# Scan block of a hybrid decoder step: cached keys turned in another batch order, and their scores issued for four batches at once

## The reference, cut to what matters

```
k_ctx = jnp.concatenate([k_buf.astype(ak.dtype), ak], axis=1)    # k_buf: 8 batches x 256 past tokens x 6 heads x 64
s = jnp.einsum('bqhd,bpqjhd->bpqhj', qblk, kg).astype(f32) * scale
...
p = jnp.exp(s - lse[..., None])
o = jnp.einsum('bpqhj,bpqjhd->bpqhd', p.astype(vg.dtype), vg).astype(f32)
```

## Time and profile before

| | |
|---|---|
| median of three runs | 2490.94 us (2488.32 to 2491.29) |
| profiled execution, first to last instruction (its span; the page gives no other time of its own) | 2483.1 us |
| what lies around the span, against that median | 7.8 us |
| PE busy | 2420.2 us, 97% |
| PEld busy | 2263.6 us, 91% |
| DVE busy | 1634.5 us, 66% |
| ACT busy | 1048.3 us, 42% |
| POOL busy | 11.4 us |
| mean rate of the DMAs | 115 GB/s |
| granted TensorE clock, mean of the span | 0.991 |

### The profile page before, as it was taken

One profiled execution on the slowest core, in us unless ns is written; L12 is line 12 of the kernel. 1 busy time (PEld: TensorE's weight loads), 2 busy tenths in 40 slices (PEclk: granted clock), 3 DMA queues, 4 the chain that ended last, 5 costly groups with the idle time before them and its releaser, 6 DMA issues. The chain is left out here.

```text
span 2483.1 us, 49073 instructions
## 1 busy us (share of the span) xinstructions
PE 2420.2 (97%) x19147; PEld 2263.6 (91%) x19147; DVE 1634.5 (66%) x2830; ACT 1048.3 (42%) x1709; POOL 11.4 (0%) x43
## 2 busy tenths in 40 slices
PE   7999999999999999999999999998999999999998
PEld 5998999899877999899999989988989689999997
DVE  8872684565857786278478538726668678846854
ACT  5541353343554554145255315424247445533532
POOL 0000000000000000000000000000000000000000
PEclk8999999999999999999999999999999999999999
DMA  8246335522233224633233553364121331322331
GB/s 307 74 137 215 109 99 184 185 78 73 69 128 96 69 77 134 213 94 96 82 86 85 161 187 97 105 214 156 44 90 52 121 120 52 99 85 81 101 87 62
DMA packets 398243, 285.67 MB, mean 115 GB/s; under 512 B 18274, under 2 KB 396440, under 8 KB 397703
## 3 DMA queue, kind: packets, MB, share of 16 engines
q1 hardware_dynamic: 397676, 283.36, 37.6%
q10 hardware_dynamic: 410, 0.18, 0.0%
HBM read 271.71 MB, written 11.79 MB: 114 GB/s over the span
## 5 line engine op out<-in xcount | busy, mean ns | idle before, releaser
L347 PE MATMUL PS<-f_xH,f_wqH 128*128 128x288 f32 x2140 | 634.9, 297 | 3.1 <-issue 3.0
L347 PE MATMUL PS<-f_xL,f_wqH 128*128 128x288 f32 x2140 | 631.8, 295 | 0.0
L347 PE MATMUL PS<-f_xH,f_wqL 128*128 128x288 f32 x2140 | 629.8, 294 | 0.0
L347 PEld LDWEIGHTS PS<-f_xH,f_wqH 128*128 128x128 f32 x2140 | 401.2, 187 | 6.0 <-issue 5.4
L347 PEld LDWEIGHTS PS<-f_xH,f_wqL 128*128 128x128 f32 x2140 | 403.3, 188 | 0.0
L347 PEld LDWEIGHTS PS<-f_xL,f_wqH 128*128 128x128 f32 x2140 | 401.9, 188 | 0.0
L347 PE MATMUL PS<-f_actH,f_wqH 128*128 128x288 f32 x1408 | 323.9, 301 | 1.3 <-DVE f_wqL L1013 1.3
L347 PE MATMUL PS<-f_actH,f_wqL 128*128 128x288 f32 x1408 | 315.4, 295 | 0.0
L347 PE MATMUL PS<-f_actL,f_wqH 128*128 128x288 f32 x1408 | 315.3, 295 | 0.0
L746 DVE SCALAR_TENSOR_TENSOR xT<-PS,modT,xT 128x288 f32<-128x288 f32 (+1 forms) x80 | 41.4, 517 | 369.2 <-PE PS L347 368.9
L347 PEld LDWEIGHTS PS<-f_actH,f_wqH 128*128 128x128 f32 x1408 | 230.2, 189 | 27.0 <-issue 25.0
(11 more groups left out here) (536 smaller groups left out, 4323.6 us busy)
## 6 DMA issues: line engine op xcount, KB each, us to landing
wslot<-in_ffn_w_in SPq DMA_DIRECT2D x176, 512.0 KB, 5.1
masks<-in_w_mod SPq DMA_DIRECT2D x42, 1536.0 KB, 6.7
wslot<-in_ffn_w_out SPq DMA_DIRECT2D x64, 384.0 KB, 4.1
wslot<-in_w_in SPq DMA_DIRECT2D x48, 512.0 KB, 4.7
wslot<-in_ffn_w_out SPq DMA_DIRECT2D x64, 320.0 KB, 3.4
setup<-in_w_mod SPq DMA_DIRECT2D x6, 1536.0 KB, 12.7
wslot<-in_w_out SPq DMA_DIRECT2D x16, 512.0 KB, 4.7
dec<-in_cache_attn_k SPq DMA_DIRECT2D x16, 384.0 KB, 3.9
```

Source lines behind the costliest of these rows:

```text
L347: ins = e.matmul(outs[j], w, x_hl[j][part], start=(start and w is wh and part == 0), stop=(stop and w is wl), skip_group_check=True)
```

## The change

There are now four buffers of turned keys instead of two: the two of `KT`, and two that lie in `h0T` and `Btm`, which the scan needs only later in the block. The cached keys are loaded in the batch order 0, 2, 4, 6, 1, 3, 5, 7, so that any four in a row belong to four different quarters of the partitions. `scores` is called twice instead of eight times; each call has twelve matmuls, of four batches in turn for each j. Their number, shapes and operands are the same in total (24 per layer). The first call stands behind `turn_keys(4)`, the second where `scores(7)` stood. `keep_keys` of the fifth to eighth turned batch wait for the first call. Two steps are also moved on TensorE: `turn_x(p+1)` now comes ahead of the second `turn_keys` of an even k.

```
+            K_ORDER = [0, 2, 4, 6, 1, 3, 5, 7]
+            KEYS = [KT[:, 0], KT[:, 1], h0T.rearrange("p a n -> p (a n)").rearrange("p (j s) -> p j s", j=NJ),
+                    Btm.rearrange("p a n -> p (a n)")[:, 0:NJ * PAST].rearrange("p (j s) -> p j s", j=NJ)]
...
-                    for b in range(4, NB):
-                        e.wait_ge(sem("ky_turned"), b - 3)
-                        e.dma_start(ring[:, b % 4], cache("cache_attn_k", b)).then_inc(ring_loaded[b % 4], 16)
+                    for i in range(4, NB):
+                        e.wait_ge(sem("ky_turned"), i - 3)
+                        e.dma_start(ring[:, i % 4], cache("cache_attn_k", K_ORDER[i])).then_inc(ring_loaded[i % 4], 16)
...
-                    def scores(b):
+                    def scores(four):
-                        if b == 0:
+                        if four == 0:
                             e.wait_ge(sem("ktok_kept"), NTT)
                             e.wait_ge(sem("qbd_ready"), 4)
-                        e.wait_ge(sem("ky_kept"), b + 1)
-                        r = slice(32 * (b // 2), 32 * (b // 2) + 32)
+                        e.wait_ge(sem("ky_kept"), 4 * four + 4)
                         for j in range(NJ):
-                            ins = e.matmul(dec_scores[r, j * PAST:(j + 1) * PAST], qbd[:, j, b % 2, r], KT[:, b % 2, j, :],
-                                           start=(b % 2 == 0 and j % 2 == 0), stop=(b % 2 == 1), skip_group_check=True)
+                            for i in range(4):
+                                b = K_ORDER[4 * four + i]
+                                r = slice(32 * (b // 2), 32 * (b // 2) + 32)
+                                ins = e.matmul(dec_scores[r, j * PAST:(j + 1) * PAST], qbd[:, j, b % 2, r], KEYS[i][:, j, :],
+                                               start=(four == 0 and j % 2 == 0), stop=(four == 1), skip_group_check=True)
                         ins.then_inc(sem("k_used"), 1)
...
-                        for b in KEYS_AT[k]:
-                            turn_keys(b)
-                            if b >= 1:
-                                scores(b - 1)
-                            if g == 1 and b == KEYS_AT[k][0]:
-                                segments(k + 1)
+                        first, second = KEYS_AT[k]
+                        turn_keys(first)
+                        if k == NKB // 2:
+                            scores(0)
+                        if g == 1:
+                            segments(k + 1)
+                        else:
+                            turn_x(p + 1)
+                        turn_keys(second)
                         if g == 0:
-                            turn_x(p + 1)
                             segments(k + 1)
                         else:
                             outputs(p)
                             local(p)
 
-                    scores(NB - 1)
+                    scores(1)
...
-                        if b >= 2:
-                            e.wait_ge(sem("k_used"), b - 1)
-                        e.activation(KT[:, b % 2, 0:2, :], PS[:, 2, :].rearrange("p (j s) -> p j s", j=2), ACT.Copy)\
+                        if b >= 4:
+                            e.wait_ge(sem("k_used"), 1)
+                        e.activation(KEYS[b % 4][:, 0:2, :], PS[:, 2, :].rearrange("p (j s) -> p j s", j=2), ACT.Copy)\
```

More of the change, by code:

```diff
@@ L2685, in cache @@
                         return A[name][bass.ds(l, 1), b].rearrange("a (s p) h d -> p (a s) (h d)", p=P)
-                    for b in range(4):
-                        e.dma_start(ring[:, b], cache("cache_attn_k", b)).then_inc(ring_loaded[b], 16)
+                    for i in range(4):
+                        e.dma_start(ring[:, i], cache("cache_attn_k", K_ORDER[i])).then_inc(ring_loaded[i], 16)
                     clear_retired(e)
@@ L3088, in keep_keys @@
                         e.wait_ge(sem("kx_turned"), b + 1)
-                        if b >= 2:
-                            e.wait_ge(sem("k_used"), b - 1)
-                        e.activation(KT[:, b % 2, 0:2, :], PS[:, 2, :].rearrange("p (j s) -> p j s", j=2), ACT.Copy)\
+                        if b >= 4:
+                            e.wait_ge(sem("k_used"), 1)
+                        e.activation(KEYS[b % 4][:, 0:2, :], PS[:, 2, :].rearrange("p (j s) -> p j s", j=2), ACT.Copy)\
                             .then_inc(sem("kx_kept"), 1)
                         e.wait_ge(sem("ky_turned"), b + 1)
-                        e.activation(KT[:, b % 2, 2, :], PS[:, 3, 0:PAST], ACT.Copy).then_inc(sem("ky_kept"), 1)
+                        e.activation(KEYS[b % 4][:, 2, :], PS[:, 3, 0:PAST], ACT.Copy).then_inc(sem("ky_kept"), 1)
                     def keep_h0(b):
```

## The result

| | before | changed |
|---|---|---|
| median, five runs each | 2490.5 us (2487.4 to 2491.29) | 2480.15 us (2478.93 to 2484.16) |
| ratio, 95% interval | | 0.9969 [0.9958, 0.9979] |
| profiled execution: span, its own time | 2483.1 us, not given | 2482.5 us, 2484.16 us |
| PE busy, granted clock | 2420.2 us, 0.991 | 2416.8 us, 0.985 |

The changed kernel is faster by 7.7 us as the ratio puts it (5.2 to 10.5) and by 10.4 us as the medians do; two more comparisons on other occasions gave 0.9956 [0.9942, 0.9969] and 0.9956 [0.9943, 0.9969], 11.0 us. The forecast was 15.1.

A forecast was written before the change was run, and what follows sets the result against it. TensorE was taken to bound the kernel, busy 97% of the span. Packing score groups, less new waits, gains 7.55 us per layer; two layers give 15.1 us, 2490.94 to 2475.8 us, range 2471 to 2482.5 us.

The forecast's parts named there:

- TensorE bounds the stretch, and DVE moves along: Scan block, keys turned and scored: TensorE sets the pace; time gained before `outputs(1)` moves DVE's whole list forward too.
- A packed group takes 1.45 us: Each of two new score groups per layer, 24 records in four quarters, takes 1.45 us, as `values` suggests.
- The first rival: Score groups: the four quarters don't overlap, a group costs 5.68 us, the run takes 2493.0 us; chance 4%.
- New waits of 0.53, 0.46 and 0.53 us: TensorE idles ahead of `segments(2)`, `turn_keys(5)` and `segments(4)`, 1.52 us per layer in all.
- The handovers: Rival: ScalarE emptying PSUM banks for `turn_keys` costs 0.56 us at all seven handovers per layer; 2481.9 us, chance 8%.
- Loads are free: Key and value loads in the scan block land before they are wanted, so they cost nothing.
- 7.55 us per layer: Gain up to `turn_x(3)` in each layer, the middle of 7.68 by timeline and 7.42 by sum.
- From `turn_x(3)` to the block's end all three lists are as before, and each is moved by the same 7.55 us, waits included: Rest of each layer's scan block: the engines' lists only shift earlier, keeping the full 7.55 us gain.
- 7.8 us above that span, and nothing outside the span changes: Whole run: the median lies 7.8 us above the profiled span, so 15.1 us comes straight off 2490.94 us.
- The third rival, the clock falls: New short idle pieces halve TensorE's clock from 723.65 to 743.95 us; 2512.8 us, chance 3%.
- The prediction's own sign of being wrong: Among the listed signs: the granted clock leaves 1.00 between 721.5 and 780 us.
- The time inside the range: Whole run: measured time lies within 2471 to 2482.5 us, allowing for other group lengths, other waits, median scatter and handovers.

The follow-up runs named there:

- The late fillers: Kernel before plus four unread filler matmuls per layer, ahead of outputs 2 and 3, the third old state and the new states: 2484.29 us, ratio 0.9979.
- the seven fillers: Changed kernel plus unread filler matmuls in seven idle places per layer, each ahead of a wait: 2469.41 us, ratio 0.9924; repeated, 2467.96 us, ratio 0.9920.
- the second profile of before: Kernel before, no edit, run and profiled again: 2490.72 us, ratio 1.0004.
- the batch-by-batch variant: Changed kernel with score-group loops swapped, one batch's three matmuls before the next: 2480.44 us; with fillers in seven idle places per layer, 2480.35 and 2477.78 us.
- nine places filled: Changed kernel with fillers in seven idle places per layer, plus ahead of segments 0 and behind `spread_inverses()`: 2467.52 us, ratio 0.9917.

## Why the prediction was wrong

- *TensorE bounds the stretch, and DVE moves along:* right. `gated(1)` starts at 741.92 us (forecast near 741.8), and its wait, 2.10 us in the earlier trace rows, is 0.68:

```profile
741.92 0.86 DVE L3293 SCALAR_TENSOR_TENSOR ssd<-ssd_in,small,PS 128x128 f32<-128x128 f32 x3 [0.68 <-PE PS L2793]
```

- *A packed group takes 1.45 us:* right, 1.43 and 1.44. The Trainium skill ("TensorE: Matmul & The Clock Gate", Part 3) gives 3.07 times for four row tiles; these are four column tiles (32 weight columns each, the outputs in four quarters of the partitions), for which it gives no figure, and they came to 5.68 / 1.43 = 3.97 times against four separate calls. The first rival's price was wrong for another reason: four batches in a row without turns take 2.80 us, not 5.68.
- *New waits of 0.53, 0.46 and 0.53 us:* right, 0.52, 0.39 and 0.52; for the third the profile names no releaser. The handovers did not become the bound.
- *Loads are free:* right; no TensorE wait on a DMA shows in the block.
- *7.55 us per layer:* a little high; 7.34 behind the second `turn_keys`, 7.35 over the part. That is 0.4 us for the run.
- *"From `turn_x(3)` to the block's end all three lists are as before, and each is moved by the same 7.55 us, waits included":* this is the step that failed. The lists are as before, but not the clock. The stretch took 46.3 us in the one profile that I had, and I carried that over. In other executions it takes up to 55.7 us in the kernel before and up to 55.9 us in the changed one.
- *"7.8 us above that span, and nothing outside the span changes":* failed with it. Only 1.7 us lie around the span. The late fillers take 5 us from the median of before (2489.4 us to 2484.3), and the seven fillers take 7 and 11 us from the changed kernel (2476.6 and 2478.8 us to 2469.4 and 2468.0). How much half clock each kernel has is also seen from the mean clocks that every run lists. A run of length T at mean clock c has lost (1 - c) x T to it. By that estimate 20 runs of before on one chip lost 26.6 us on their mean, and five of the changed kernel 30.7 us; on another chip it was 27.4 and 31.7 us. So the change brought about 4 us more of half clock, and 15.1 - 0.4 - 4 = 10.7 us is near the 11.0 us of those two comparisons. In the five runs of the result, at 0.9864, the loss was 33.7 us, some 7 us more than before's elsewhere, which fits the 7.7 us there. The clocks are listed to 0.001, or 2.5 us of a run, so only means of several runs bear such a reading.
- *The third rival, the clock falls:* it had 3%, and it is what happened, though in another place and at a smaller price. The rival was priced for 723 to 744 us, where the change adds idle time, and in this profile the clock stayed at 1.00 there. It fell beside waits of 0.55 and 0.30 us that were there before. The prediction's own sign of being wrong, a clock that leaves 1.00 between 721.5 and 780 us, does catch it. Its argument against the rival, that an idle piece of 0.56 us had left the clock at 1.00, came from one execution: in the second profile of before the clock fell behind an idle piece of the same length. (The 18.5 us of work in the rival's price should be 18.8: 20.3 us less 1.52 us of waits.)
- *The time inside the range:* luck in part. 2480.15 us lies in it because the range allowed for other waits and for groups of another length, none of which came; half clock has no term in it.

Shown: that the late stretches lose up to 9.6 us each to half clock while the part that was changed gains what was forecast, that the kernel before has such losses too, and that filling idle pieces makes both kernels faster and raises their mean clock. Also shown, by the clocks listed for the runs, is that the changed kernel has more half clock than the one before: 0.9871 on the mean of its 15 runs on three occasions, none above 0.990, against 0.9894 on the mean of 74 runs of before, which reach 0.992. The profiles agree, but few executions were traced: a late stretch of over 50 us is one of four in the two profiles of the kernel before and four of six in the three of the changed kernel. Open is why the changed kernel has more of it, why the falls differ between executions, and why fillers did so little for the batch-by-batch variant (2480.4 us without them, 2480.4 and 2477.8 with them).

## What to carry to other kernels

A profile is one execution. Before it is used as the base of a sum, its own time has to be put beside the runs: a span 7.8 us under the median was a sign that this execution lacked something that the median has, as only 1.7 us of it lay outside the span. Where light matmuls and transposes with short idle pieces stand in a row at full clock, expect other executions in which the clock is not full, and price a gain there with and without it. Filler matmuls about as long as an idle piece that cannot be removed cost almost nothing (28.71 against 28.41 us in the first stretch), and here they were worth 7 to 11 us beside the change's 8 to 11: 2469.4 and 2468.0 us together, against 2489.2 us before. They are to be tried and not relied on: in the batch-by-batch variant they gave 0 and 3 us in two tries, and pieces of half clock stayed in every kernel with them.

## What the hardware showed unexpectedly

- The same stretch of instructions took from 46.3 to 55.9 us, differently from one execution to the next, and from one layer to the next in the same execution, with a mean granted clock from 1.00 down to 0.79.
- With nine places filled, the wait of 1.44 us among them, no half clock followed that wait (1.00, where one run with seven fillers had a mean of 0.79 over 8 us), but a piece of it stood earlier in each layer, at a mean of 0.57 over 4 us, behind a wait that was filled too.
- Matmuls of 32 weight columns overlapped with the next ones in another quarter of the partitions even where each quarter's three stand together: 2.80 us for four batches, against 1.42 us for one and 1.43 us for four in turn.
